# Stick-breaking attention: the pair's output product directly behind the next piece's scores

## The reference

```python
z = jnp.einsum('bhqd,bhkd->bhqk', qb, kp) * scale          # scores against all keys up to the block's end
log_keep = jnp.where(strict, jax.nn.log_sigmoid(-z), 0.0)
rev = lax.cumsum(log_keep, axis=3, reverse=True)
after = jnp.concatenate([rev[..., 1:], zeros], axis=-1)
w = jnp.where(strict, jnp.exp(jax.nn.log_sigmoid(z) + after), 0.0)
outs.append(jnp.einsum('bhqk,bhkd->bhqd', w, vp))           # the output product
```

## Time and profile before

| what | value |
|---|---|
| runs, median (lowest to highest) | 1220.19 us (1219.93 to 1221.82) |
| profiled execution, its own time | 1221.61 us |
| its span in the trace | 1219.8 us |
| TensorE (PE) busy | 1190.9 us, 98% |
| VectorE / ScalarE / GpSimd busy | 410.4 / 420.2 / 522.1 us |
| chain that ended last | PE 90%, DVE 5%, ACT 2%, DMA 1% |
| loop over the pieces of layer 1 | about 653 to 819 us |

### The profile page before, as it was taken

One profiled execution on the slowest core, in us unless ns is written; L12 is line 12 of the kernel. 1 busy time (PEld: TensorE's weight loads), 2 busy tenths in 40 slices (PEclk: granted clock), 3 DMA queues, 4 the chain that ended last, 5 costly groups with the idle time before them and its releaser, 6 DMA issues.

```text
span 1219.8 us, 14965 instructions
## 1 busy us (share of the span) xinstructions
PE 1190.9 (98%) x6221; PEld 970.4 (80%) x6221; DVE 410.4 (34%) x661; ACT 420.2 (34%) x577; POOL 522.1 (43%) x270
## 2 busy tenths in 40 slices
PE   7999999999999999999999999999999999999996
PEld 6887768988888888888887777667988888888885
DVE  8369452811111110000705877747211110110007
ACT  6344664332222322212235554523432232321220
POOL 6897514344444445443354223113544444444440
PEclk9999999999999999999999999899999999999999
DMA  8632315252333323323242211102533333323311
GB/s 211 180 88 72 103 43 198 69 145 87 104 101 89 104 87 103 104 88 103 94 120 84 65 53 55 50 8 79 158 102 90 100 104 88 102 91 102 102 52 69
DMA packets 152643, 117.30 MB, mean 96 GB/s; under 512 B 18689, under 2 KB 138537, under 8 KB 152577
## 3 DMA queue, kind: packets, MB, share of 16 engines
q1 hardware_dynamic: 152576, 116.36, 32.6%
HBM read 112.00 MB, written 3.17 MB: 94 GB/s over the span
## 4 chain that ended last, share of the span: by engine, by line
PE 90%; DVE 5%; ACT 2%; DMA 1%; issue 1%; POOL 0%; SPq 0%; DVEq 0%; ACTq 0%
PE ps L1473 17%; PE ps L1475 17%; PE ps L1474 17%; PE ps L1495 9%; PE ps L1496 9%; PE ps L1497 9%; PE ps L1918 2%; PE ps L1894 1%; PE ps L1905 1%; DMA raw<-in_even_w_in 1%; PE ps L1934 1%; PE ps L1503 1%; PE ps L1936 1%; PE ps L1935 1%; DVE stats L1347 1%
## 5 line engine op out<-in xcount | busy, mean ns | idle before, releaser
L567 POOL TENSOR_TENSOR wlo<-raw,whi 128x1024 fp32r<-128x1024 f32 x189 | 454.2, 2407 | 641.3 <-ACT whi L670 640.6
L1473 PE MATMUL ps<-xhi,whi 128*128 128x512 f32 (+1 forms) x1000 | 379.5, 379 | 0.9 <-ACT uP L714 0.9
L1475 PE MATMUL ps<-xhi,wlo 128*128 128x512 f32 (+1 forms) x1000 | 374.2, 374 | 0.0
L1474 PE MATMUL ps<-xlo,whi 128*128 128x512 f32 (+1 forms) x1000 | 374.2, 374 | 0.0
L670 ACT CAST whi<-raw 128x1024 fp32r<-128x1024 f32 x189 | 199.5, 1061 | 216.9 <-PE ps L1497 180.6
L1473 PEld LDWEIGHTS ps<-xhi,whi 128*128 128x128 f32 x1000 | 188.2, 188 | 42.2 <-issue 6.4
L1475 PEld LDWEIGHTS ps<-xhi,wlo 128*128 128x128 f32 x1000 | 188.3, 188 | 34.0
L1474 PEld LDWEIGHTS ps<-xlo,whi 128*128 128x128 f32 x1000 | 188.4, 188 | 32.2
L1016 DVE TENSOR_TENSOR gt<-ps,sg 128x512 f32<-128x512 f32 x44 | 30.4, 692 | 372.6 <-PE ps L1475 372.6
L1495 PE MATMUL ps<-whi,ghi 128*128 128x512 f32 x352 | 137.1, 390 | 0.0
L1497 PE MATMUL ps<-whi,glo 128*128 128x512 f32 x352 | 137.0, 389 | 0.0
(11 more groups left out here) (217 smaller groups left out, 1065.8 us busy)
## 6 DMA issues: line engine op xcount, KB each, us to landing
raw<-in_ffn_w SPq DMA_DIRECT2D x132, 512.0 KB, 3.7
raw<-in_odd_w_in SPq DMA_DIRECT2D x24, 512.0 KB, 3.9
raw<-in_even_w_in SPq DMA_DIRECT2D x16, 512.0 KB, 5.1
h<-in_x SPq DMA_DIRECT2D x8, 512.0 KB, 5.1
raw<-in_even_w_out SPq DMA_DIRECT2D x8, 512.0 KB, 3.7
raw<-in_odd_w_out SPq DMA_DIRECT2D x8, 512.0 KB, 3.6
bias<-rel_scratch SPq DMA_DIRECT2D x8, 256.0 KB, 4.2
out<-h SPq DMA_DIRECT2D x3, 512.0 KB, 2.6
```

The lines of the kernel that those rows point to most:

```text
L567: eng.tensor_tensor(lo, raw_of(b), hi, ALU.subtract).then_inc(w_lo, 1)
L1473: eng.matmul(o_, w_hi_, x_hi_, start=start, stop=False)
L1474: eng.matmul(o_, w_hi_, x_lo_, start=False, stop=False)
L1475: return eng.matmul(o_, w_lo_, x_hi_, start=False, stop=stop)
```

## The change

In TensorE's loop, `stick_out` moves from behind the first run of the projection (and behind the first early sum) to directly behind `stick_scores(n + 1)`. The instructions are the same; only their order on TensorE differs. ScalarE's, VectorE's, GpSimd's and SyncE's programs are unchanged.

```diff
                 if n + 1 < PIECES:
                     stick_scores(n + 1)
                 early = EARLY_AT.get(n, ())
+                if n >= 4 and n % 3 == 1:
+                    stick_out((n - 4) // 3)
                 if runs:
                     oqk(*runs[0])
                 if early:
                     early_part(early[0])
-                if n >= 4 and n % 3 == 1:
-                    stick_out((n - 4) // 3)
                 if 0 <= n - 1 < PIECES:
                     stick_turn(n - 1)
                 if runs[1:]:
```

## The result

The changed kernel is slower: median 1225.89 us (1223.33 to 1226.32, 5 runs) against 1220.44 us of the kernel before (1219.93 to 1221.82, 5 runs), ratio 1.0037 with a 95% interval of 1.0026 to 1.0048. That is +4.5 us (3.2 to 5.9). The ratio goes by the means of the runs; the medians are 5.5 apart. The forecast was +2.5. I had given 0.50 to slower by more than 0.2%. The median of 1220.19 us that the forecast started from, times the ratio, is 1224.7 us: inside my range of 1219.5 to 1225.4, but above the 1223.6 at which my own case ended. The plain median of the changed kernel stands 0.5 us above the range. The forecast size was about half of the measured one.

What follows compares the result with a forecast made beforehand. TensorE, busy 98% of the span, was taken as the bound. Six pairs at 0.46 us (2.76) less 0.30 at the seventh point made +2.46, on the median 1220.19: 1222.7 us, range 1219.5 to 1225.4.

Steps and rivals of the forecast that it cites:

- my own case: The forecast without its rivals, 1222.7 us, with a range of its own of 1222.1 to 1223.6; chance 0.60.
- The hidden relay: Behind odd projection tiles: ScalarE's rounding and VectorE's lowering need 1.80 us, transposes cover 1.20; new 0.60 us wait before scores.
- The sum for a pair: From one pair's scores to the next's, 8.00 us against 7.54: +0.46, from +0.60 wait and −0.14 shorter path; six times.
- The direct step between the two kinds of tiles: 64x128 to 128x64 tiles, between scores and product, unseen in the trace: taken like other changes, bounds 0.10 less or more.
- The seventh point: Pair 6, where an early sum stands in place of the projection tile: −0.30 us, bounded on the other side by zero.
- The second wait, for `pair_out`: Rival: the even projection tile also waits for ScalarE's copy at five tiles, up to 0.5 us each: 1225.2 us; chance 0.10.
- The DMA and GpSimd work for the weights hangs on `w_used`: Weight loading and casting inside a pair: its signal comes 2.3 us later, claimed to cost nothing.
- inherited in full: After the last of six slower pairs, the chain from scores to early sums takes over the whole 2.76 us delay.
- The clock: Rival: between 785.10 and 791.50 us the clock stays at 2.4 GHz, giving back 3.1 us: 1219.6 us; chance 0.10.

Runs made afterwards that it cites:

- e10: Kernel before, with ScalarE rounding the next weight block ahead of an odd projection tile instead of behind it; ratio 1.0012 to the kernel before, +1.5 us.
- e11: Changed kernel, with ScalarE rounding the next weight block ahead of an odd projection tile instead of behind it; ratio 1.0083 to the kernel before, +10.1 us.
- e5: Kernel before, with the output product moved the opposite way, behind the transposes; ratio 0.999 to the kernel before, −1.2 us.
- e1: Kernel before, with only the products of pairs 0 to 4 moved behind the scores; ratio 1.0016 to the kernel before, +2.0 us.
- e2: Kernel before, with only the product of pair 5 moved behind the scores; ratio 1.0018 to the kernel before, +2.2 us.
- e4: Changed kernel, with the weight block rounded behind projection tile 15 rounded after the loop instead; ratio 1.0015 to the kernel before, +1.8 us.
- e12: Kernel before, unaltered, measured against itself; ratio 1.0002.
- e9: Changed kernel, unaltered, measured a second time against the kernel before; ratio 1.0041.
- e3: Kernel before, with only the product of pair 6 moved behind the scores; ratio 0.9996 to the kernel before.

## Why the prediction was half right

- *The hidden relay.* Right, in place and mechanism. The scores start at t0+1.80, as worked out, and e10 and e11 show that TensorE pays for that relay only in the new order. The sum for a pair was 0.46 and measured 0.42 (S+7.96 for S+8.00); the projection part takes 3.31 instead of 3.35. Six pairs: 2.76 forecast, 2.45 measured in A.
- *The direct step between the two kinds of tiles.* I took it as any other change of tiling, and it was; the product starts at S+0.54 for S+0.55. The Trainium skill (TensorEngine Tiling (Array Packing), Key Properties: changing the mode drains TensorE) points the right way, and e5 shows the gain where the relay stays hidden.
- *The seventh point.* −0.30 forecast; −0.30 measured up to the second early sum (6.65 for 6.95), −0.2 to −0.3 over all of C.
- *The second wait, for `pair_out`.* It didn't occur: 0.25 us in hand (705.35 to 705.60), forecast 0.16.
- *"The DMA and GpSimd work for the weights hangs on `w_used`, which comes 2.3 us later within the pair but blocks are cast five tiles ahead: nothing."* This is the step that failed. The blocks are indeed not needed sooner. But the moved signal moves GpSimd's 2.4 us onto VectorE's scan of 256 columns, which then takes 2.8 us instead of 1.3. At pairs 0 to 4 there is slack behind it, and e1 shows no cost. At pair 5 the lowering of the mixer's output queues behind the scan, and TensorE waits for that: +0.9 us (e2, e4). So *"inherited in full"* was too little as well. The trace of before held the evidence, at a place that I hadn't looked at for this (two scans that take 1.26 us alone):

```profile
666.60 2.40 POOL L567 TENSOR_TENSOR wlo<-raw,whi 128x1024 fp32r<-128x1024 f32 x1 [3.47 <-ACT whi L670]
...
667.48 2.65 DVE L1402 TENSOR_TENSOR_SCAN wq<-keep,gt 128x256 f32<-128x256 f32 x2
```

It even stood in the pair that I had read: the scan of 384 columns at 695.87 took 2.97 us beside GpSimd (695.65 to 698.04), and the next of that size, at 699.09, took 0.93.

- *The clock.* I had it as a rival that gives time back, 3.1 us, on the ground that nothing shortens the standstill. The whole fall is worth 2.1, as e12 shows, and I didn't ask what a longer standstill does. The three traces with the long one (after, e9, e2) have 6, 12 and 11 matmuls at 1.2 GHz and a mean B of 15.71 us. The eight with the early sum's distance at 6.03 to 6.05 (before, e12, e1, e3, e4, e5, e10, e11) have 12, 0, 7, 0, 7, 7, 6 and 7 and a mean of 14.13. The difference of 1.6 us holds the 0.9 of the standstill and some 0.7 of clock.

The account by the traces: 2.45 in A, 1.6 in B, −0.3 in C make +3.7 us, against measured intervals of 3.2 to 5.9 and 3.5 to 6.6. The 0.7 is a mean over draws.

The mean granted clock of every execution, traced or not, says more. At 0.996 the changed kernel took 1223.3, 1223.7 and 1224.3 us, and the kernel before a median of 1221.1 (64 of its 102 executions in the four comparisons): +2.6. At 0.994 it is 1226.3 (seven executions) against 1223.5 (13): +2.8. So at the same clock the change costs 2.6 to 2.8 us, near the 3.1 of A, the standstill and C. The rest goes with the clock, since more executions had the lower one: seven of ten of the changed kernel stood at 0.994, and 20 of 102 of the kernel before at 0.994 or lower. Between 0.994 and 0.996 lie 2.4 us in the kernel before (1223.5 against 1221.1), so an estimate is half of that, 1.2 us.

The longer standstill seems to have a part in it. In the kernels that have it (after, e9, e2) 18 of 22 executions stood at 0.995 or lower; in those with the short one (the kernel before in the four comparisons, e1, e3, e4, e5, e10, e11, e12) 52 of 176. So a low mean clock came more often with the longer standstill. Not shown is where in an execution the clock fell: a fall at 164 us counts in the same mean, and it isn't the change's. e4, which undoes only the standstill's growth, takes 2.7 to 3.2 us off the time and 0.9 off the path, so the growth seems to be worth more than its length; the intervals are too wide to say by how much.

That the measured time came to lie in my range is in part luck. Its upper end stood there for the second wait, which didn't occur; what filled the gap was the standstill's growth, put at nothing, and the clock, which I had only expected to give time back.

## What to carry to other kernels

Before moving a piece of work, ask what it hides: here 3.3 us of products and transposes stood between a tile's end and its reader, and covered a relay of 1.8 us over two engines. With the 2.3 us of products gone the transposes alone didn't. Moving it the other way, behind the transposes, saved the same change of tiling without baring the relay.

A signal that comes later moves other engines' work too, even where nobody waits for it. Check what that work now lies beside, and follow it into the one iteration where the usual slack is missing.

## What the hardware showed

- VectorE's scan and GpSimd's subtraction don't share: the first scan started at 705.69, GpSimd's instruction ended at 707.35, the scan ended at 707.89, 0.54 us later, where a scan of this size takes about 0.65 in all. It had waited. The Trainium skill (SBUF — State Buffer, Who interferes with whom) says that a VectorE instruction with two SBUF inputs contends with a GpSimd one that reads SBUF. It calls the lock on the port pair that the two share exclusive. This scan reads two SBUF inputs, and the trace agrees: 2.20 us beside GpSimd's instruction, about 0.65 alone.
- The same program after the same standstill of 2.5 us ran 12, or 0, of the following matmuls at 1.2 GHz (0.66 and 1.00 mean granted clock over 10 us). One profile can't give the price of such a stretch. The fall of 12 cost 2.1 us. A standstill of 1.8 us, at 164 us, was followed by 1.2 GHz in five of 14 traces.
- A change of tiling costs about 0.1 us in front of it (0.32 between starts in place of 0.23) and 0.1 behind it (0.33, as from 699.59 in the changed kernel to the next matmul at 699.92); one change less was worth 0.17 us in e5.
